# Thirteen early expert tiles as split fp32r products, their low parts made by adding DMAs, in a two-layer encoder with product-key experts

## The reference

```python
def peer(h, w_q, subkeys, u_tab, v_tab):
    q = (hf @ w_q).astype(jnp.float32).reshape(t, PEER_HEADS, 2, PEER_QDIM // 2)
    s = jnp.einsum('thsd,hskd->thsk', q, subkeys.astype(jnp.float32))
    top_s, top_i = lax.top_k(s, PEER_TOPK)
    ...
    best_s, best_pos = lax.top_k(cand_s.reshape(...), PEER_TOPK)
    expert = jnp.take_along_axis(cand_i.reshape(...), best_pos, axis=-1)
    gate = jax.nn.softmax(best_s, axis=-1)
    ...
        act = jax.nn.gelu(jnp.einsum('thkd,td->thk', ub, hb).astype(jnp.float32))
        return jnp.einsum('thk,thkd->td', (gb * act).astype(vb.dtype), vb)
```

## Time and profile before

| | |
|---|---|
| median of 3 runs | 2107.4 us |
| profiled execution, its own time | 2106.16 us |
| its span | 2104.4 us |
| PE busy | 2034.0 us, 97% |
| PEld busy | 1755.5 us, 83% |
| DVE busy | 1580.0 us, 75% |
| ACT busy | 973.5 us, 46% |
| POOL busy | 262.6 us, 12% |
| mean granted clock of TensorE | 0.996 |
| chain that ended last | PE 69%, DVE 20%, issue 4%, DMA 3%, ACT 2% |

### The profile page before, as it was taken

One profiled execution on the slowest core, in us unless ns is written; L12 is line 12 of the kernel. 1 busy time (PEld: TensorE's weight loads), 2 busy tenths in 40 slices (PEclk: granted clock), 3 DMA queues, 4 the chain that ended last, 5 costly groups with the idle time before them and its releaser, 6 DMA issues.

```text
span 2104.4 us, 33858 instructions
## 1 busy us (share of the span) xinstructions
PE 2034.0 (97%) x11364; PEld 1755.5 (83%) x11364; DVE 1580.0 (75%) x3436; ACT 973.5 (46%) x1619; POOL 262.6 (12%) x309
## 2 busy tenths in 40 slices
PE   5999999999999999999999999899999999999998
PEld 5898988888888888888788989887888888888877
DVE  8884898767888888887657369886666667678854
ACT  3223347655444444444522242685555555544443
POOL 2003439200000000000010051780000000000000
PEclk9999999999999999999999999999999999999999
DMA  9467311355778877555453362115555565555561
GB/s 372 146 258 263 117 54 61 128 186 200 273 277 307 301 271 277 191 184 193 164 174 105 131 239 83 57 53 175 197 182 196 197 221 191 194 184 179 179 235 59
DMA packets 115742, 392.22 MB, mean 186 GB/s; under 512 B 12752, under 2 KB 20816, under 8 KB 115152
## 3 DMA queue, kind: packets, MB, share of 16 engines
q1 hardware_dynamic: 115664, 391.21, 52.2%
HBM read 384.35 MB, written 6.82 MB: 186 GB/s over the span
## 4 chain that ended last, share of the span: by engine, by line
PE 69%; DVE 20%; issue 4%; DMA 3%; ACT 2%; SPq 1%; DVEq 1%; POOL 0%; POOLq 0%; ACTq 0%
PE ps L905 25%; PE ps L896 13%; PE ps L898 6%; PE ps L867 4%; PE ps L639 4%; DVE v_lo L1710 4%; PE ps L652 3%; PE ps L781 3%; DVE next_w_ada_ring L1755 3%; DVE u_lo L1705 2%; PE ps L875 2%; DVE gated L1718 1%; DMA weight_ring<-in_w_q_dram 1%; ACT gelu L1258 1%; PE ps L807 1%
## 5 line engine op out<-in xcount | busy, mean ns | idle before, releaser
L896 PE MATMUL ps<-h_hi_lo,u_hi 128*128 128x512 f32 x1728 | 630.7, 399 | 6.3 <-DVE u_lo L1705 5.8
L898 PE MATMUL ps<-h_hi_lo,u_lo 128*128 128x256 f32 x1512 | 425.9, 282 | 0.0
L896 PEld LDWEIGHTS ps<-h_hi_lo,u_hi 128*128 128x128 f32 x1728 | 326.3, 189 | 76.6 <-issue 6.5
L898 PEld LDWEIGHTS ps<-h_hi_lo,u_lo 128*128 128x128 f32 x1512 | 287.4, 190 | 8.2
L905 PE MATMUL ps<-v_hi,gated_hi 128*128 128x512 f32 x864 | 272.2, 396 | 4.8 <-DVE gated_lo L1724 3.8
L1705 DVE TENSOR_TENSOR u_lo<-weight_ring,u_hi 128x1024 fp32r<-128x1024 f32 x216 | 263.6, 1221 | 14.5 <-ACT u_hi L1247 11.2
L905 PE MATMUL ps<-v_lo,gated_hi 128*128 128x512 f32 x864 | 268.5, 392 | 0.0
L905 PE MATMUL ps<-v_hi,gated_lo 128*128 128x512 f32 x864 | 266.6, 390 | 0.0
L1710 DVE TENSOR_TENSOR v_lo<-weight_ring,v_hi 128x1024 fp32r<-128x1024 f32 x216 | 263.2, 1219 | 0.5 <-ACT v_hi L1252 0.5
L1252 ACT ACTIVATE v_hi<-weight_ring 128x1024 fp32r<-128x1024 f32 x216 | 227.4, 1053 | 54.8 <-PE ps L905 54.6
L1258 ACT ACTIVATE gelu<-gelu 128x256 f32<-128x256 f32 x216 | 90.3, 418 | 329.4 <-DVE gelu L1714 329.4
(11 more groups left out here) (316 smaller groups left out, 3138.9 us busy)
## 6 DMA issues: line engine op xcount, KB each, us to landing
weight_ring<-in_u_tab_dram SPq DMA_DIRECT2D x224, 512.0 KB, 4.4
weight_ring<-in_v_tab_dram SPq DMA_DIRECT2D x216, 512.0 KB, 3.5
next_w_ada_ring<-in_w_ada_dram SPq DMA_DIRECT2D x56, 512.0 KB, 4.4
weight_ring<-in_w_in_dram SPq DMA_DIRECT2D x46, 512.0 KB, 3.7
w_ada_ring<-in_w_ada_dram SPq DMA_DIRECT2D x40, 512.0 KB, 9.0
v_tail<-in_v_tab_dram SPq DMA_DIRECT2D x40, 512.0 KB, 4.8
weight_ring<-in_w_q_dram SPq DMA_DIRECT2D x32, 512.0 KB, 3.5
u_ahead<-in_u_tab_dram SPq DMA_DIRECT2D x22, 512.0 KB, 8.9
```

Source lines behind the costliest of these rows:

```text
L896: last = mm(both, UH[:, b, k, :], HB[:, :, k, :], start=(k == 0), stop=(k == KT - 1))
L898: mm(PS[:, 4 + b, 0:T], UL[:, b, k, :], HH[:, k, :], start=False, stop=False)
```

## The change

Thirteen tiles, not eleven, are early in the top-16 stage, so AHEAD is 22 and NM is 106; `gate_ahead` covers tiles 82 to 103, and the plain expert tiles behind it vanish but for the last two. Each of the thirteen becomes three fp32r products with HH and HL. Its high part and a negated copy are made by ScalarE (`cut_ahead`): both are copies of the raw tile into fp32r buffers, the second with scale -1. Then GpSimd issues a DMA that adds the raw tile from DRAM onto the negated copy (`add_raw`), which leaves the low part. There are 3 raw buffers, 6 places for high parts and 6 for low ones. SyncE loads the first three raw tiles; ScalarE issues the load of tile a+2 from its own DMA queue at the head of `cut_ahead(a)`. The cuts of tiles 0 to 7 stand at n = 1, 3, 5, 7, 9, 10, 12, 15 of the query loop, those of 8 to 12 behind the GELUs of tiles 4 to 8. H32, which the nine late tiles still need, is written later, behind the GELUs of tiles 9 and 10. DVE's written-out passes of one-hots become a loop. The v ring's places in memory change, their number doesn't.

```diff
-A_TOP = 11
-A_RING = 11
+A_TOP = 13
+A_RING = 3
...
+CUT_AT = (1, 3, 5, 7, 9, 10, 12, 15)
...
+        AHEAD_PLACE = (0, 1, 2, 3, 0, 1, 2, 3, 4, 5, 0, 1, 2)
...
-                        for a in range(A_TOP):
-                            sp.dma_start(RAWU[a][:, :, :], u_tab[l, NM + a].rearrange("p (k n) -> p k n", n=P)).then_inc(in_ahead[a // 2], 16)
+                        for a in range(A_RING):
+                            ahead_raw(a)
...
                 def ahead(a):
-                    pe.wait_ge(*ahead_loaded(l, a))
-                    if a == 0:
-                        pe.wait_ge(h32_done, l + 1)
+                    pe.wait_ge(*ahead_summed(l, a))
                     if a >= 2:
                         pe.wait_ge(ahead_gelu, l * AHEAD + a - 1)
+                    hi, lo, out = UAH[AHEAD_PLACE[a]], UAL[AHEAD_PLACE[a]], PS[:, 2 + a % 2, 0:T]
                     for k in range(KT):
-                        last = mm(PS[:, 2 + a % 2, 0:T], RAWU[a][:, k, :], H32[:, k, :], start=(k == 0), stop=(k == KT - 1))
+                        mm(out, hi[:, k, :], HH[:, k, :], start=(k == 0), stop=False)
+                        mm(out, hi[:, k, :], HL[:, k, :], start=False, stop=False)
+                        last = mm(out, lo[:, k, :], HH[:, k, :], start=False, stop=(k == KT - 1))
                     last.then_inc(ahead_mm, 1)
...
+                def add_raw(a):
+                    pool.wait_ge(ahead_cut, l * A_TOP + a + 1)
+                    place = AHEAD_PLACE[a]
+                    gp.dma_start(UAL[place][:, :, :], u_tab[l, NM + a].rearrange("p (k n) -> p k n", n=P),
+                                 accum_op=ALU.add).then_inc(ahead_low[place], 16)
...
+                    if n - 3 in CUT_AT:
+                        add_raw(CUT_AT.index(n - 3))
+                for a in range(7, A_TOP):
+                    add_raw(a)
...
+                def cut_ahead(a):
+
+                    place = AHEAD_PLACE[a]
+                    act.wait_ge(*ahead_loaded(l, a))
+                    if place >= 4:
+                        act.wait_ge(q_mm, l * 16 + 20 - place)
+                    elif a >= 4:
+                        before = max(b for b in range(a) if AHEAD_PLACE[b] == place)
+                        act.wait_ge(ahead_mm, l * AHEAD + before + 1)
+                    if a and a + 2 < A_TOP:
+                        act.wait_ge(ahead_cut, l * A_TOP + a)
+                        nc.scalar.dma_start(RAWU[(a + 2) % A_RING][:, :, :], u_tab[l, NM + a + 2].rearrange(
+                            "p (k n) -> p k n", n=P)).then_inc(in_ahead[(a + 2) % A_RING], 16)
+                    fn(UAH[place][:, :, :], RAWU[a % A_RING][:, :, :], ACT.Copy)
+                    fn(UAL[place][:, :, :], RAWU[a % A_RING][:, :, :], ACT.Copy, scale=-1.0).then_inc(ahead_cut, 1)
...
-                gelu_ahead(4)
-                gelu_ahead(5)
+                for a in range(4, 9):
+                    gelu_ahead(a)
+                    cut_ahead(a + 4)
                 act.wait_ge(gate_in, l + 1)
                 fn(GATE[:, :, :], GATE[:, :, :], ACT.Exp).then_inc(gate_exp, 1)
-                for a in range(6, A_TOP):
+                for a in range(9, A_TOP):
                     gelu_ahead(a)
+                    if a < 11:
+                        for k in range(4 * (a - 9), 4 * (a - 9) + 4):
+                            last = fn(H32[:, k, :], HT[:, k, :], ACT.Identity, bias=MODS[l][:, SH2, k:k + 1])
+                        if a == 10:
+                            last.then_inc(h32_done, 1)
...
-                for i in range(1, 8):
+                with dve.Fori(1, 8) as i:
```

More of the change, by code:

```diff
@@ L191, in trunk @@
         GER = at("gelu_back", 5120, [P, AHEAD, T])
-        GHA = at("gated_ahead_hi", 10240, [P, AHEAD, T], F32R)
-        GLA = at("gated_ahead_lo", 15360, [P, AHEAD, T], F32R)
-        V_AT = (0, 1024, 2048, 3072, 4096, 20480, 21504, 22528, 23552)
+        GHA = at("gated_ahead_hi", 10752, [P, AHEAD, T], F32R)
+        GLA = at("gated_ahead_lo", 16384, [P, AHEAD, T], F32R)
+        V_AT = range(0, 1024 * TAIL_RING, 1024)
         RAWV = [at(f"v_tail_{a}", o, [P, D]) for a, o in enumerate(V_AT)]
@@ L339, in trunk @@
         s_sum = sem("expert_scores_summed")
-        in_ahead = [sem(f"u_ahead_pair_loaded_{a}") for a in range((A_RING + 1) // 2)]
+        in_ahead = [sem(f"u_ahead_loaded_{a}") for a in range(A_RING)]
+        ahead_cut = sem("u_ahead_hi_and_negated_done")
+        ahead_low = [sem(f"u_ahead_low_summed_{i}") for i in range(6)]
         in_late = [sem(f"u_ahead_late_loaded_{i}") for i in range(2)]
@@ L375, in trunk, with ahead_summed @@
         LATE_STORES = [len(range(i, A_GATE, 4)) for i in range(4)]
+        AHEAD_PLACE = (0, 1, 2, 3, 0, 1, 2, 3, 4, 5, 0, 1, 2)
         def ahead_loaded(l, a):
-            pair = a % A_RING // 2
-            tiles = [b // A_RING for b in range(A_TOP) if b % A_RING // 2 == pair]
-            return in_ahead[pair], 16 * (l * len(tiles) + sum(b <= a // A_RING for b in tiles))
+            return in_ahead[a % A_RING], 16 * (l * len(range(a % A_RING, A_TOP, A_RING)) + a // A_RING + 1)
+        def ahead_summed(l, a):
+            place = AHEAD_PLACE[a]
+            return ahead_low[place], 16 * (l * AHEAD_PLACE.count(place) + AHEAD_PLACE[:a + 1].count(place))
         TILE_IN, TILE_OUT, TILE_Q = 0, IN_TILES, IN_TILES + KT
@@ L877, in ahead_step @@
                         last.then_inc(ahead_mm, 1)
+                pe.wait_ge(h32_done, l + 1)
                 for k in range(KT):
@@ L1780, in _ @@
                         gate_ahead(i * 2 + b)
-                expert_tiles(AHEAD_TILE + AHEAD, NM - 2)
+                if AHEAD_TILE + AHEAD < NM - 2:
+                    expert_tiles(AHEAD_TILE + AHEAD, NM - 2)
                 u_low(E0 + NM - 1, 1)
```

15 lines of the change are left out of this document (9 added, 6 removed).

## The result

The changed kernel takes 2089.95 us (median of 4 runs, 2087.16 to 2091.07) against 2106.67 us before on the same chip: ratio 0.9918, 95% interval 0.9903 to 0.9932. The forecast was 2091. The profiled execution has a span of 2089.1 us, 15.3 us shorter than before; the sum of the prediction said 15.3 too. That agreement is luck: the table shows where the time went, by events that both traces have. Two gains came in about the size foretold and a little larger, the loss was nine times the one foretold, and one stretch moved the other way.

What follows compares the result with a forecast made beforehand. Bounds: TensorE in the expert loop, DVE also where it gates; in the top-16 stage a load hole, then TensorE (layer 0) or DVE held by GpSimd (layer 1). From 2106.2: -10.3 - 8 + 1 + 2 = -15.3, 2091 us; range 2083 to 2105.

Steps and rivals of the forecast that it cites:

- Two tiles out of the loop: Expert loop: AHEAD 20 to 22, NM 108 to 106 saves 5.1 us per layer, -10.3 us for two layers.
- The hole and TensorE: Top-16 stage, query loop: earlier w_q load and cheaper TensorE work gain 4.0 us per layer (2.5 to 6), -8 us.
- The hole: Top-16 stage start: w_q tile 4's load waits behind eleven u_ahead loads; removing that takes 2.5 us off each layer.
- each cheaper product: Query loop, TensorE: an early tile takes 2.87 us as three fp32r products, not 3.48 in fp32; four save 2.4 us.
- Rival C: Query loop: GpSimd's eight more DMAs hold DVE 0.8 us each, 6.4 per layer; 2104 us, chance 0.08.
- The feed: Early tiles behind the queries: late low parts cost 0.5 us per layer, +1 us; called the uncertain term.
- D: Time from a cut's end to the adding DMA's landing, GpSimd's part included: taken as 6 us, between 3.5 and 13.7.
- The 3.2 us: Trainium skill's estimate for a 512 KB GpSimd-issued DMA; by it the feed costs nothing, the sum 1 us lower.
- T0: End of key_scores(15), the last query's key scores; 11.2 us before the gates when DVE leads, 9.5 where TensorE leads.
- Rival A: Early tiles behind the queries: feed slow but bearable, D about 10, 4.9 us late per layer; 2100 us, chance 0.15.
- The loop: Stage of gates: DVE's one-hots in a loop pay 0.15 us per wait for register addresses, +2 us (0 to 6).
- Rival B: Tiles 7 to 11: D at 13.7, GELU, cut and add in series, slower than before; 2114 us, chance 0.10.

Runs made afterwards that it cites:

- b_spread: Kernel before, with three u_ahead loads ahead of w_q tile 4 and the other eight one by one behind w_q tiles 4 to 11: 2098.9 us, ratio 0.9965.

## Why the prediction came out right, point by point

**Two tiles out of the loop: right.** -11.0 us for -10.3. The steps are the foretold ones (v halves 5.79 us apart at 862, 22 of them; 5.55 in the loop). Some 0.4 us per layer more came off than the steps account for; no run looked into that.

**The hole and TensorE: the sum right, the reasons half.** -9.8 for -8. The hole went, and it was worth 3.3 and 3.6 us per layer (b_spread), not the 2.5 of its own step. In layer 0 all 11.3 us of VectorE's waits for TensorE go with it, and its additions take 7.7 us more; in layer 1 the 2.9 us ahead of n=2 go, and 0.8 of additions. The 0.6 us that the prediction gave to each cheaper product shows in no wait, since b_spread has none with the old products. The prediction was right that layer 0 would come to look like layer 1, clashes and all; that they are 1.4 us per layer shorter than in b_spread was in no term. Rival C (0.8 us of VectorE lost to each of the eight adding DMAs) did not happen.

**The feed: wrong, and the step that failed is the value of D.** The prediction wrote that in the crowd a load costs 1.2 us of moving and an adding one 1.2 more, and took D = 6 because few loads run behind the queries. In truth the change itself fills the queues: 1.71 us for the raw load, 2.86 for the adding one, 2.7 for the store, against 2.87 us of TensorE per tile. D is 9.1 us for tile 8 of layer 0 (260.73 to 269.81), 11.6 and 11.4 for tiles 9 and 10, and 11.8 for tile 10 of layer 1 (1291.86 to 1303.61). The 3.2 us that the prediction has for the landing of such a DMA, beside its sum, were not met either: no adding DMA of the changed kernel lands in under 5.4 us.

One D for all tiles was wrong too. The prediction's line for tile 8 (T0 + 17.2 + D against T0 + 24.2) gives 2.1 us late with 9.1; the rest is that tiles 9 and 10 land later still. Rival A's formula (9.1 + 2D - 24.2) would give 3.1 to 8.5 us, around the measured 4.6 and 4.4, but it counts D twice because tile 7 is late in it. Tile 7 was not: its D is 5.7 us, and it landed 2.3 us before its turn. So a loss of rival A's size happened, by another path and for another reason than the ones written beside it. TensorE's stretches at 1.2 GHz were in no term, and cost next to nothing here.

**The loop: wrong in sign.** +2 predicted, -3.8 measured where it is the only edit. The 0.1 us for a register address is real; the step that failed is that it was added to a stage whose passes were taken as rigid. In the changed kernel's own profile 1.1 us of the 3.8 are missing again, by the longer stretch at the lower clock in layer 1.

**What nothing hid or cost.** ScalarE's DMA issues took 0.33 to 0.39 us and GpSimd's mostly 0.86; in the query loop neither shows on the chain, as booked. Behind it one issue of ScalarE per layer (0.33 us) stands on the chain, ahead of the late cut. H32 and the larger last store stand in no wait of TensorE or ScalarE.

**So why 2091?** Feed and loop were off by +8.1 and -4.7, the two gains by -0.7 and -1.8, and 0.9 came off outside. With the right loss of the feed and all else as written the forecast would have been 2099; the loop and the larger gains brought it back. Rival B (slower) needed D above 11.6 for tile 7 and again for tile 11; in layer 0 they had 5.7 and 9.3.
